# Low parts of mixer weights by an accumulating transfer after a negative rounding on ScalarE, instead of a GpSimd subtraction

## The reference, cut to what matters

```python
proj = h @ w_in                                   # first block, 1024 x 3072
z = jnp.einsum("bld,de->ble", u, w_in)            # second block, 1024 x 2824
...
return y @ w_out
```

## Time and profile before

| | us |
|---|---|
| two timed executions, median | 3358.68 |
| lowest, highest | 3355.98, 3361.39 |
| span of the profiled execution | 3359.5 |
| PE busy in it | 3304.6 |
| POOL busy in it | 289.8 |

### The profile page before, as it was taken

How to read it: one execution, slowest core, us unless ns; L and a number is a source line. 1 busy time by engine, 2 the same in 40 slices (tenths; PEclk the granted TensorE clock), 3 DMA queues, 4 the chain that set the end, 5 groups by cost and what they waited for, 6 DMA issues and landing times.

```text
span 3359.5 us, 56027 instructions
## 1 busy us (share of the span) xinstructions
PE 3304.6 (98%) x22342; PEld 2941.2 (88%) x22342; DVE 2065.5 (61%) x2942; ACT 1504.9 (45%) x2508; POOL 289.8 (9%) x157
## 2 busy tenths in 40 slices
PE   8999999999999999999999999999999999999999
PEld 7887876788889888876788889889999998899998
DVE  6882556678627882556678726746665277476643
ACT  5342445543335342445553334565443254754432
POOL 1000022100000000022100001210000022100000
PEclk9999999999999999999999999999999999999999
DMA  4343321233333332321233332212223322122222
GB/s 120 100 125 102 106 57 57 70 91 98 97 98 88 100 99 92 105 59 55 70 89 99 93 102 76 57 47 78 93 87 96 102 68 55 57 82 91 90 88 88
DMA packets 330747, 287.62 MB, mean 86 GB/s; under 512 B 9697, under 2 KB 326201, under 8 KB 330581
## 3 DMA queue, kind: packets, MB, share of 16 engines
q1 hardware_dynamic: 330117, 284.17, 28.2%
q10 hardware_dynamic: 464, 1.10, 0.1%
HBM read 283.10 MB, written 5.27 MB: 86 GB/s over the span
## 4 chain that ended last, share of the span: by engine, by line
PE 90%; DVE 5%; ACT 3%; DMA 1%; issue 1%; ACTq 0%; SPq 0%; DVEq 0%
PE ps L647 18%; PE ps L648 18%; PE ps L649 18%; PE ps L698 6%; PE ps L700 6%; PE ps L699 6%; PE ps L753 2%; PE ps L2113 2%; PE ps L2115 2%; PE ps L2114 2%; PE ps L1698 1%; PE ps L757 1%; PE ps L1737 1%; PE ps L1722 1%; PE ps L2163 1%
## 5 line engine op out<-in xcount | busy, mean ns | idle before, releaser
L639 DVE TENSOR_TENSOR wlo<-raw,whi 128x1024 fp32r<-128x1024 f32 (+1 forms) x412 | 495.2, 1202 | 753.0 <-ACT whi L632 750.0
L632 ACT ACTIVATE whi<-raw 128x1024 fp32r<-128x1024 f32 (+1 forms) x493 | 511.6, 1040 | 946.7 <-PE ps L649 790.4
L647 PE MATMUL ps<-xhi,whi 128*128 128x512 f32 (+2 forms) x2576 | 864.5, 336 | 2.0 <-DVE wlo L639 2.0
L648 PE MATMUL ps<-xlo,whi 128*128 128x512 f32 (+2 forms) x2576 | 853.1, 331 | 0.0
L649 PE MATMUL ps<-xhi,wlo 128*128 128x512 f32 (+2 forms) x2576 | 850.6, 330 | 0.0
L647 PEld LDWEIGHTS ps<-xhi,whi 128*128 128x128 f32 x2576 | 485.9, 189 | 65.0 <-issue 17.5
L649 PEld LDWEIGHTS ps<-xhi,wlo 128*128 128x128 f32 x2576 | 484.5, 188 | 47.8
L648 PEld LDWEIGHTS ps<-xlo,whi 128*128 128x128 f32 x2576 | 485.6, 188 | 42.0 <-issue 0.5
L647 PE MATMUL ps<-hhi,whi 128*128 128x512 f32 (+2 forms) x1056 | 359.0, 340 | 0.7 <-issue 0.7
L648 PE MATMUL ps<-hlo,whi 128*128 128x512 f32 (+2 forms) x1056 | 358.1, 339 | 0.0
L649 PE MATMUL ps<-hhi,wlo 128*128 128x512 f32 (+2 forms) x1056 | 357.7, 339 | 0.0
(11 more groups left out here) (322 smaller groups left out, 6714.9 us busy)
## 6 DMA issues: line engine op xcount, KB each, us to landing
raw<-in_ffn_w_up_dram SPq DMA_DIRECT2D x176, 512.0 KB, 3.7
raw<-in_ffn_w_down_dram SPq DMA_DIRECT2D x120, 512.0 KB, 3.5
raw<-in_w_in_dram SPq DMA_DIRECT2D x94, 512.0 KB, 3.8
raw<-in_ffn_w_gate_dram SPq DMA_DIRECT2D x88, 512.0 KB, 3.8
raw<-in_w_out_dram SPq DMA_DIRECT2D x32, 512.0 KB, 3.4
raw<-in_ffn_w_down_dram SPq DMA_DIRECT2D x24, 256.0 KB, 2.8
tbias_scratch<-rev_scratch SPq DMA_DIRECT2D x1, 3072.0 KB
y<-tbias_scratch SPq DMA_DIRECT2D x6, 512.0 KB, 4.7
```

The lines of the kernel that those rows point to most:

```text
L632: act.activation(into[:, 0:n], raw[slot][:, 0:n], ACT.Copy).then_inc(b.s.weights_hi, 1)
L639: eng.tensor_tensor(lo[:, 0:n], raw[slot][:, 0:n], hi[:, 0:n].bitcast(F32), ALU.subtract).then_inc(b.s.weights_split, 1)
L647: pe.matmul(o, wh, hi[:, t0:t0 + w], start=first, stop=False)
L648: pe.matmul(o, wh, lo[:, t0:t0 + w], start=False, stop=False)
```

## The change

For the same eighty granules (5 to 24 of each mixer) POOL no longer subtracts. ACT makes two passes over the raw weights: first the **negative** rounded weights into `wlo` (Copy with scale -1), then the rounded weights into `whi` as before. POOL then issues a transfer from `raw` to `wlo` that adds to what is there, so that `wlo` becomes `raw - whi`; it waits until that transfer has landed and then adds one to `weights_split`. Waits of ACT for the landed load and for the free slot stand ahead of the first of its two passes.

```diff
+        def split_hi_neg(act, b, g, g2, slot, n=1024):
+            act.wait_ge(b.s.weights_landed[slot], 16 * g2 + 16)
+            act.wait_ge(b.s.granules_done, g + 1)
+            act.activation(wlo[slot][:, 0:n], raw[slot][:, 0:n], ACT.Copy, scale=-1.0).then_inc(b.s.weights_neg, 1)
+            act.activation(whi[slot][:, 0:n], raw[slot][:, 0:n], ACT.Copy).then_inc(b.s.weights_hi, 1)
+
+        def add_lo(pool, b, count, g, slot, n=1024, handover=False):
+            if handover:
+                pool.wait_ge(b.s.weights_split, g + CR)
+            pool.wait_ge(b.s.weights_neg, count + 1)
+            pool.wait_ge(b.s.weights_hi, g + 1)
+            pool.dma_start(wlo[slot][:, 0:n], raw[slot][:, 0:n], accum_op=ALU.add).then_inc(b.s.weights_added, 16)
+            pool.wait_ge(b.s.weights_added, 16 * count + 16)
+            pool.sem_inc(b.s.weights_split, 1)
...
             def hi_split(g):
-                split_hi(act, b, mgb(l) + g, mgb2(l) + g // 2, g % 2)
+                (split_hi_neg if 5 <= g < 25 else split_hi)(act, b, mgb(l) + g, mgb2(l) + g // 2, g % 2)
...
             for g in range(5, 25):
-                split_lo(pool, b1, mgb(l) + g, g % 2, handover=(g == 5))
+                add_lo(pool, b1, 20 * l + g - 5, mgb(l) + g, g % 2, handover=(g == 5))
```

More of the change, by code:

```diff
@@ L490, in semaphores @@
             s.weights_split = sem(f"{b}_weights_split")
+            s.weights_neg = sem(f"{b}_weights_neg")
+            s.weights_added = sem(f"{b}_weights_added")
             s.granules_done = sem(f"{b}_granules_done")
@@ L2308, in hi_split @@
             def hi_split(g):
-                split_hi(act, b, g2b(l) + g, g2b2(l) + g // 2, g % 2, n_of(g))
+                (split_hi_neg if 5 <= g < SPLIT2_DVE else split_hi)(act, b, g2b(l) + g, g2b2(l) + g // 2, g % 2, n_of(g))
             hi_split(3)
@@ L2673, in pool_mix2 @@
             for g in range(5, SPLIT2_DVE):
-                split_lo(pool, b2, g2b(l) + g, g % 2, n_of(g), handover=(g == 5))
+                add_lo(pool, b2, (SPLIT2_DVE - 5) * l + g - 5, g2b(l) + g, g % 2, n_of(g), handover=(g == 5))
         KIND_AT = ["f1", "m1", "f2"] * LAYERS + ["m2", "f"] * LAYERS
```

## The result

The changed kernel took 3392.30 us (median of two executions) against 3358.68: ratio 1.0095, interval 1.0066 to 1.0124. A second comparison on another chip, with four executions against fifteen, gave 3393.31 against 3354.95: ratio 1.0120, interval 1.0104 to 1.0136. So the change costs 1.0 to 1.2%, 34 to 38 us. I had forecast 3442, 83 us more, with a range from 3388: the time lies inside the range, but only just, and the loss is 0.4 of the one forecast.

What follows compares the result with a forecast made beforehand. The prediction took TensorE's work plus its few gaps to bound the kernel. 3359.5 us plus 70 for late low parts, 8 for ScalarE's queue and 5 for the clock gave 3442 us, range 3388 to 3565.

Steps and rivals of the forecast that it cites:

- What bounds the kernel: Whole kernel: TensorE, busy 3304.6 of 3359.5 us, sets the time with its gaps; freeing GpSimd gains nothing by itself.
- the term for late low parts: All four mixers: TensorE waits for granules whose later low part exceeds its slack, 70 us in 34 waits.
- L: Each granule's chain: ScalarE's last pass to the count TensorE waits for, put at 6.5 us, ends 3.8 and 10.6.
- The table from slacks to waits: Mixers: eighty slacks (GpSimd's subtraction end to first matmul) turned into waits per L: 14 us at 3.8, 264 at 10.6.
- ScalarE's queue: First block's mixers mainly: copies of transposed probabilities behind the two passes start 1.04 us later; 8 us, ends 0 and 12.
- The clock: Mixers: half of the six waits over 4 us bring a clock fall of 1.5 us each; 5 us, ends 0 and 51.
- The load queue: SP's load of the slot's next granule, issued later by the low part's delay, stays covered by 2 us.
- The short transfer: Rival: the transfer chain takes 3.8 to 6.0 us, giving 3378 to 3425, centre 3400, not slower by 2%; chance 0.37.
- My own sum from the loads: Forecast case, L between 6 and 9: 3.8 us load, 1.5 second reading, 1.2 GpSimd's part make 6.5; chance 0.41.
- The long transfer: Rival: L of 9 us or more through slow adding, interfering loads or GpSimd held up; 3565 to some 3650; chance 0.12.
- every wait bring the clock down: Rival: each of TensorE's waits lowers its clock, 46 us more than in the sum, some 3490; chance 0.08.
- nothing was gained: Rival: no wait or a gain, if GpSimd now delays VectorE and that matters; 2.0 us to win; chance 0.02.

Runs made afterwards that it cites:

- plain_copy: Changed kernel with GpSimd's transfer only copying the raw weights, adding nothing (low parts wrong): 3372.38 us, ratio 1.0049.
- picked: Changed kernel with only 62 of 80 granules, those whose slack covers the later low part, going the new way, others subtracted as before: 3364.86 us, ratio 1.0030.
- picked_second: Against picked, the first block's mixers put back as before, leaving twelve granules in each of the second block's mixers: 3357.17 us, ratio 1.0003.

## Why the prediction was wrong in size, point by point

*What bounds the kernel* held. TensorE's gaps make the loss, and GpSimd's 133 us of freed time bought nothing.

*The step that failed is the term for late low parts, 70 us of the 83, and in it L first of all*, the time from ScalarE's last pass to the count, which I had put at 6.5 us. Taken from the trace of the changed kernel it is 5.1 us, the median of all eighty; at granule 5 it is 5.14, which with 0.05 to the matmul makes the 5.19 of the rows. Two of its three terms were too large. The base was taken from loads that come from memory, 3.8 us for 512 KB; a plain transfer by GpSimd between buffers on the chip lands in 2.9. GpSimd's own part was taken as 1.2 us; it is 0.6 from ScalarE's end to the issue. The third, 1.5 us for the second reading, was right in size: 1.6 by plain_copy. At 5.0 us the prediction's table gives 32 us of waits in place of 70, so L alone accounts for 38 us of the error.

*The table from slacks to waits* held in its shape and was too high in every run. The rows show 22.9 us behind GpSimd's count, in 15 places, where it gives 32; 161 where it gives 226; 11.5 for 15, 7.5 for 10, 7.6 for 14. The rows at granule 6 of the second block's first mixer show why. A rounding that starts ahead of TensorE's wait for the granule before is not moved by that wait, and the granule gets the slack back; for this I had taken the order of the old trace. There the rounding of granule 6 started at 2068.10, behind the first matmul of granule 5 at 2066.71, so I counted no slack back, which is how the prediction came to waits of 4.5, 4.3 and 3.3 us in a row although it says that waits come on every second granule. In the changed kernel the pair for granule 6 starts at 2075.80, released by TensorE, and the waiting matmul of granule 5 comes only at 2078.37. So granule 6 waited for 1.1 us in the first of these mixers and not at all in the second, where the table at 5.0 us has 2.8; granule 11 waited in neither, where it has 1.4. The places were right as far as they go: of the longest waits, which were to be at granules 5, 6 and 10 of the second block's mixers, 5 and 10 are there (2.7 and 3.1 us in the first, 4.0 and 2.8 in the second).

*Two things in L that I had not seen.* GpSimd issues the next transfer only after the one before has landed. I wrote that nothing else stands in its queue, but its own wait does. At 2078.92 the issue for granule 6 stands behind the landing of granule 5's (its row above names that transfer as what ended 4.29 us of idle time). It happened four times, at granules 6 and 11 of the second block's mixers, and made these issues 0.6 to 2.1 us later; only one of the four granules made TensorE wait at all, for 1.1 us. And the landing varies: 18 of the eighty transfers took more than 5.0 us, 12 of them in the second block's mixers, up to 6.5 us. The one of granule 5 in the last mixer took 5.9 us, and TensorE's wait there is the longest, 4.0 us. Of the 17 transfers that ran beside a load for more than 1 us the median is 5.1 us, of the 51 that met no load 4.5; but there are slow ones among these too (up to 5.9 us), so the cause is open.

*ScalarE's queue*: I took 8 us, of a possible 12. The waits that name ScalarE grew by 7 us, and the times of picked against picked_second give 9, all in the first block, where the comparison of starts had put it.

*The clock*: I took 5 us. In the profiled execution after, the stretches at the lower level last 31 us in all, before 25, so this pair shows 3 us. But which stretches fall is not the same from one execution to the next, as the 14 us at 2235 before show, and a single profile cannot size this term. All executions do better: in the second comparison the mean granted clock of the changed kernel is 0.992 to 0.995 (median 0.994), that of before 0.996 to 0.999 (median 0.998). A difference of 0.004 over 3390 us is an estimate of 14 us. So the term was too small there, and 21 us for the count, 7 for ScalarE's queue and 14 for the clock make 42 us, near the 38 measured there.

*The load queue*: loads of `raw` still land in 3.8 us, and none of ScalarE's waits ahead of the new passes names a load; held.

*The rivals.* The short transfer is what came: L = 5.0, centre 3400, to which I had given 0.37 against 0.61 for slower by over 2%. That its 3400 lies only 7 us from the time is partly luck, as its waits are 9 us too many and its clock too small. By the page "DMA: Bandwidth & Descriptors" of the Trainium skill (section "Anatomy of one DMA") a transfer from GpSimd takes 2.0 us and its bytes at 436 GB/s; for 1 MB of reading that is an estimate of 4.4 us, and the trace has 4.5. For the plain copy it gives an estimate of 3.2 us against 2.9 in the trace. My own sum from the loads had 0.41. The two rested on the same rows; what parted them was an allowance for GpSimd that no row supported, and the assumption that a transfer between buffers on the chip costs as much as one from memory. The long transfer did not come: the longest L of the eighty is 8.0 us, under the 9 of that case. Of the lock that the Trainium skill's page "SBUF — State Buffer" describes (section "SBUF: two separate sides"), the issues show nothing: GpSimd's instruction takes 859 to 1016 ns in all eighty. Nor did every wait bring the clock down, and nothing was gained.

*What can be told apart.* I called 67 us about the least that could be told from none. The intervals above are some 10 and 5 us wide on either side, so the loss of 34 to 38 us is real.

## What to carry to other kernels

Before a step on a hidden chain is made longer, list the slack of every instance, not the sum: eighty steps that were all hidden had 0.1 to 15.5 us, and eighteen of those with little carried most of the loss. Ask also whether the order of the old trace, from which such a list is taken, survives the change. The price of lateness is then a table over L, flat at first and steep later (34 to 38 us with one transfer, some 200 more for the second), so the effort belongs into L. A nearest row should be near in kind as well (memory or on chip, pieces of which size), and where the result hangs on one such number, both ends deserve a case of equal weight. And work that replaces another engine's puts a wait into the queue of the engine that issues it.

## What the runs showed of the hardware that I had not expected

VectorE's instructions became shorter where GpSimd no longer subtracted: 84 us less busy time than before, 39 of them in the steps shown here. The convolution's steps in the second block's mixers, before and after (ns min/median/max):

```profile
L2562 DVE SCALAR_TENSOR_TENSOR m_aconv<-m_apad,par,m_aconv x120: 752/759/2976, 2089.2 to 2843.4; 128x528 f32<-128x528 f32 x120
```

```profile
L2583 DVE SCALAR_TENSOR_TENSOR m_aconv<-m_apad,par,m_aconv x120: 757/762/769, 2103.3 to 2871.0; 128x528 f32<-128x528 f32 x120
```

The medians are equal within 3 ns, and the longest falls from 2976 to 769 ns. Before, 20 of the 120 steps took over 0.8 us, and each of them ran beside a subtraction of GpSimd; two steps and a subtraction of the kernel before:

```profile
2176.24 3.65 DVE L2562 SCALAR_TENSOR_TENSOR m_aconv<-m_apad,par,m_aconv 128x528 f32<-128x528 f32 x2
2176.26 2.39 POOL L639 TENSOR_TENSOR wlo<-raw,whi 128x1024 fp32r<-128x1024 f32 x1 [13.51 <-ACT whi L632]
```

The first of the two steps is the one of 2976 ns, 2.2 us over the median, beside a subtraction of 2.39 us: it looks as if the step had stood still until the subtraction was over. It goes the other way too: where one of these steps had started first, the subtraction took 2.5 to 2.8 us, against a median of 2.4. TensorE's waits for VectorE are 17.7 us before and 15.0 after, so little of the 84 us reached the time. An adding transfer in flight does not do this: 63 of the 120 steps of the changed kernel ran beside one, and none took over 769 ns.
